# The down projection of a decoder layer: two of three token tiles by seven block products a unit, taken by groups of chunks

## The reference

```python
up = rmsnorm(x, g_ffn) @ w_up
upc, ffn_buf_new = causal_conv(ffn_buf, up, ffn_conv_w)
u, gt = jnp.split(upc, 2, axis=-1)
x = x + (jax.nn.silu(gt) * u) @ w_down        # w_down: 2816 x 1024
...
y_prompt = rmsnorm(xp, g_final)
```

## Time and profile before

| | us |
|---|---|
| median of 3 runs | 1082.9 |
| the profiled execution, its own time | 1084.21 |
| the profiled execution, span from first to last instruction | 1082.5 |
| up stage, products of L2078 | 378.8 to 814.4 |
| down stage, plain pairs of L2102 | 814.4 to 1041.1 |
| last pair and final norm | 1041.1 to 1082.5 |

### The profile page before, as it was taken

One profiled execution on the slowest core, in us unless ns is written; L12 is line 12 of the kernel. 1 busy time (PEld: TensorE's weight loads), 2 busy tenths in 40 slices (PEclk: granted clock), 3 DMA queues, 4 the chain that ended last, 5 costly groups with the idle time before them and its releaser, 6 DMA issues.

```text
span 1082.5 us, 17576 instructions
## 1 busy us (share of the span) xinstructions
PE 1060.4 (98%) x6746; PEld 1029.0 (95%) x6746; DVE 787.0 (73%) x1310; ACT 512.0 (47%) x880; POOL 43.5 (4%) x165
## 2 busy tenths in 40 slices
PE   7999999999999999999999999999999999999995
PEld 7999988888999999999999999999999999999994
DVE  6954788898899987778778768777777454454457
ACT  7444345665444554454454444444445333333354
POOL 0100000000000000000000000000000000000004
PEclk9999999999999999999999999999999999999998
DMA  7211201113544113112212211311336867556404
GB/s 259 96 40 45 97 21 40 38 61 144 152 130 141 62 59 118 59 59 98 78 59 84 93 59 62 115 59 60 106 128 210 285 199 221 178 180 198 146 1 157
DMA packets 47395, 119.09 MB, mean 110 GB/s; under 512 B 5040, under 2 KB 25392, under 8 KB 47280
## 3 DMA queue, kind: packets, MB, share of 16 engines
q1 hardware_dynamic: 43904, 113.59, 31.8%
q10 hardware_dynamic: 3408, 4.38, 1.1%
HBM read 98.33 MB, written 20.66 MB: 110 GB/s over the span
## 4 chain that ended last, share of the span: by engine, by line
PE 65%; DVE 4%; issue 2%; ACT 1%; DVEq 0%; ACTq 0%
PE psum L2078 40%; PE psum L2102 21%; PE psum L2054 2%; PE psum L1833 1%; DVE x_sb L1488 1%; DVE zb L1145 1%; DVE zb L1787 0%; PE psum L2135 0%; DVE att L1481 0%; DVE x_sb L1495 0%; DVE h_lo L1499 0%; DVE x_sb L1505 0%; ACT psum L1100 0%; DVE act_lo L1151 0%; DVE h_lo L1453 0%
## 5 line engine op out<-in xcount | busy, mean ns | idle before, releaser
L2078 PE MATMUL psum<-h_hi,w_lo 128*128 128x344 f32 x336 | 107.4, 320 | 0.0
L2078 PE MATMUL psum<-h_hi,act_lo 128*128 128x344 f32 x336 | 107.3, 319 | 0.0
L2078 PE MATMUL psum<-h_hi,act_hi 128*128 128x344 f32 x336 | 107.3, 319 | 0.0
L2078 PE MATMUL psum<-h_hi,w_hi 128*128 128x344 f32 x336 | 107.3, 319 | 0.0
L2078 PE MATMUL psum<-h_lo,act_hi 128*128 128x344 f32 x336 | 107.2, 319 | 0.0
L2078 PE MATMUL psum<-h_lo,w_hi 128*128 128x344 f32 x336 | 107.1, 319 | 0.0
L1151 DVE TENSOR_TENSOR w_lo<-raw,w_hi 128x1024 fp32r<-128x1024 f32 x50 | 61.1, 1224 | 59.8 <-ACT w_hi L727 59.7
L727 ACT ACTIVATE w_hi<-raw 128x1024 fp32r<-128x1024 f32 x51 | 53.8, 1056 | 83.5 <-PE psum L2102 63.5
L2102 PE MATMUL psum<-h_hi,act_hi 128*128 128x344 f32 x240 | 77.1, 321 | 0.0
L2102 PE MATMUL psum<-h_hi,w_hi 128*128 128x344 f32 x240 | 76.9, 320 | 0.0
L2102 PE MATMUL psum<-h_lo,w_hi 128*128 128x344 f32 x240 | 76.7, 320 | 0.0
(11 more groups left out here) (313 smaller groups left out, 3033.3 us busy)
## 6 DMA issues: line engine op xcount, KB each, us to landing
raw<-in_w SPq DMA_DIRECT2D x111, 512.0 KB, 3.7
att<-in_w SPq DMA_DIRECT2D x26, 512.0 KB, 4.5
act_d<-att SPq DMA_DIRECT2D x20, 516.0 KB, 2.7
zb<-act_d SPq DMA_DIRECT2D x30, 344.0 KB, 4.2
x_sb<-in_x SPq DMA_DIRECT2D x8, 516.0 KB, 5.0
x_d<-x_sb ACTq DMA_DIRECT2D x12, 344.0 KB, 2.5
x_sb<-x_d SPq DMA_DIRECT2D x3, 1376.0 KB, 7.9
out_y<-x_sb SPq DMA_DIRECT2D x12, 344.0 KB, 2.5
```

The costliest lines, as they stand in the source:

```text
L2078: ins = mm(bank[to], a, b, start=(fresh and k == p == 0), stop=(k == HALF - 1 and p == 2), skip_group_check=True)
```

## The change

Tiles 0 and 1 of the down projection are made by seven block products, tile 2 stays plain. The 11 chunk pairs form three groups of 4, 3 and 4 pairs.

- A **unit** u is one group and two row blocks m: it loads two slots (first chunks and second chunks of the group's pairs, two row blocks wide), forms four weight sums, splits seven weight parts, and makes seven products of 3 x (pairs in the group) matmuls. It uses three banks; p1 is copied with its sign changed by ScalarE into the second bank (`preload`), and VectorE reads six times into `x_sb` (`s_read`). 12 units in all.
- A **T pair** tp is tile 2, plain, for one group and two row blocks: two slots, two banks, two reads. 12 in all.
- The order is T 0-3, units 0-3, T 4-5, units 4-7, T 6-7, units 8-11, T 8-11.
- The data of a group are nine operands (b11, b21, b22, D1 to D4, and two halves of tile 2), each in two **items**; 54 items of up to 344 KB go through the same three stage buffers. All activations are stored, with the differences: `pair_diffs` makes these on VectorE (four instructions of 344 columns a pair), and the store has three rows of 516 KB a pair. The weight loads now read runs of 256 floats instead of whole rows of 1024.
- The final norm of tiles 0 and 1 runs inside units 8-11, that of tile 2 at the end.

The core of the diff, with the order of each engine around the first units:

```diff
+GROUP_PAIRS = (4, 3, 4)
+T_PAIRS = (range(0, 4), range(4, 6), range(6, 8), range(8, 12))
+S_UNITS = (range(0, 4), range(4, 8), range(8, 12), range(0))
+S_ORDER = ("p1", "p5", "p6", "p2", "p7", "p3", "p4")
...
 sync engine
-            for i in range(3):
-                load_act(i)
-            for i in range(2, DOWNS + 1):
...
+            for n in range(4):
+                load_item(n)
+            for q in (4, 5, 6):
+                load_down(q)
+            load_item(4)
+            load_item(5)
+            load_down(7)
+            store_pair(NG - 1)
+            load_item(6)
+            load_item(7)
+            load_down(8)
+            sp.wait_ge(act_stored, 32 * NG)
+            sp.wait_ge(state_out, 2 * NF)
+            sp.dma_start(x_sb[:, :, tile(2)], x2_d[:, :, tile(2)]).then_inc(x2_last_back, 16)
+            for n in range(8, 18):
+                load_item(n)
+                if n in (9, 11, 13):
+                    load_down(9 + (n - 9) // 2)
+                if n in (12, 15):
+                    load_x2((n - 12) // 3)
...
+            def load_item(n):
+                if n < 3:
+                    sp.wait_ge(part_lo_ready, parts_by(NF - 1))
+                else:
+                    sp.wait_ge(act_split, n - 2)
...
 ScalarE
+            t_hi(2, 0)
+            item_hi(4)
+            item_hi(5)
...
+            s_hi(0, "a11")
+            s_hi(0, "S1")
+            item_hi(12)
+            item_hi(13)
+            s_hi(0, "S2")
+            s_hi(0, "a12")
+            item_hi(14)
+            item_hi(15)
+            item_hi(16)
+            item_hi(17)
+            s_hi(0, "S3")
+            s_hi(0, "S4")
+            nc.scalar.activation(small[:, 62:63], eps[:, 0:1], ACT.Sqrt)
+            for g in range(3):
+                for u in S_UNITS[g]:
+                    s_hi(u, "a22")
+                    preload(u)
...
 VectorE, last chunk of the up stage
-                    w_lo_ffn(DOWN_SLOT0)
+                    item_lo(0)
+                    t_lo(0, 0)
                 act_mult(n - 1)
                 read_v3(n)
...
 VectorE, last unit of groups 0 and 1
+                        s_read(u, "p5")
+                        t_lo(T_PAIRS[g + 1][0], 0)
+                        s_read(u, "p6")
+                            item_lo(item + 2)
+                            item_lo(item + 3)
+                        s_read(u, "p2")
+                            item_lo(item + 4)
+                            item_lo(item + 5)
+                        t_lo(T_PAIRS[g + 1][0], 1)
+                        s_read(u, "p7")
...
 VectorE, between groups
+                    unit_sums(u)
+                    item_lo(item + 2)
+                    item_lo(item + 3)
+                    for n, part in ((4, "a11"), (5, "S1")):
+                        item_lo(item + n)
+                        s_lo(u, part)
+                    t_read(ta, 0)
+                    t_read(ta, 1)
...
 TensorE
+            def s_product(u, p):
+                pe.wait_ge(down_lo, SPLIT_N["S", u, part])
+                if u % 4 == 0:
+                    pe.wait_ge(act_split, X_N[group_of(u), x, 1])
+                if p == "p1":
+                    pe.wait_ge(down_read, BANK_FREE["S", u, 0])
+                if p == "p5":
+                    pe.wait_ge(down_read, BANK_FREE["S", u, 2])
+                if p == "p6":
+                    pe.wait_ge(preloaded, u + 1)
+                if p in ("p7", "p3", "p4"):
+                    pe.wait_ge(down_read, READ_N["S", u, {"p7": "p6", "p3": "p5", "p4": "p7"}[p]])
```

More of the change, by code:

```diff
@@ new lines, in numbered, with group_of, t_place, s_output @@
+def numbered(items):
+    return {x: n + 1 for n, x in enumerate(items)}
+def group_of(n):
+    return n // 4
+def t_place(tp):
+    f = next(f for f in range(4) if tp in T_PAIRS[f])
+    return f, tp - T_PAIRS[f][0]
+def s_output(u, p):
+    m1, m2 = 2 * (u % 4), 2 * (u % 4) + 1
+    return {"p2": (m1, 0), "p6": (m1, 1), "p3": (m1, 1), "p5": (m2, 1), "p7": (m2, 1), "p4": (m2, 0)}[p]
+LOADS = phases(lambda tp: [("T", tp, c) for c in range(2)], lambda u: [("S", u, c) for c in range(2)])
+LOAD_AT = numbered(LOADS)
@@ new lines, with halves_of, split_used @@
+X_ITEMS = x_items(0, T_X) + x_items(0, S_X) + x_items(1, T_X) + x_items(1, S_X) + x_items(2, S_X) + x_items(2, T_X)
+X_N = numbered(X_ITEMS)
+def halves_of(split):
+    kind, n, x = split
+    if kind == "S":
+        return (S_PARTS.index(x),)
+    e = (2 * t_place(n)[1] + x) % 4
+    return 2 * e, 2 * e + 1
+def split_used(split):
+    kind, n, x = split
+    if kind == "T":
+        return DONE_N["T", n, ("c0", "m1")[x]]
+    return DONE_N["S", n, next(p for p in S_ORDER if PRODUCTS[p][0] == x)]
@@ new lines, in home_free, with bank_free @@
+def home_free():
+    user, free = {}, {}
+    for split in SPLITS:
+        free[split] = max(split_used(user[h]) if h in user else 0 for h in halves_of(split))
+        for h in halves_of(split):
+            user[h] = split
+    return free
+def bank_free():
+    last, free = {}, {}
+    for key in phases(lambda tp: [("T", tp, i) for i in range(2)], lambda u: [("S", u, b) for b in range(3)]):
+        kind, n, i = key
+        b = T_BANKS[n][i] if kind == "T" else S_BANKS[n % 2][i]
+        free[key] = last.get(b, 0)
+        last[b] = READ_N[key] if kind == "T" else READ_N["S", n, ("p2", "p4", "p3")[i]]
+    return free
@@ L248, in landed_at @@
 def landed_at(s):
-    return 16 * sum(raw_of(r) == raw_of(s) for r in range(s + 1))
+    return 16 * sum((2 if r >= DOWN_SLOT0 and group_of(LOADS[r - DOWN_SLOT0][1]) == 2 else 1)
+                    for r in range(s + 1) if raw_of(r) == raw_of(s))
 def split_at(s):
@@ L1130, in _ @@
+            for m in (4, 5):
+                last_gain(m)
+            last_square(6)
+            last_square(7)
+            last_gain(6)
+            fin_root(2)
+            last_gain(7)
         @block.vector
@@ L1757, in _ @@
                 else:
-                    act_rest(1)
+                    t_lo(0, 1)
+                    item_lo(3)
                 read_c21(n)
@@ L1762, in _ @@
                 else:
[L1763 removed]
+                    t_lo(1, 0)
+                if n % 2 == 0:
+                    pair_diffs(n // 2 - 1)
             read_c12(NF - 1)
             tap_1(NF - 1, 1)
[L1766 removed]
+            t_lo(1, 1)
             tap_2(NF - 1, 1)
@@ L1813, in _ @@
-            fin_add(NT - 1, 5)
-            dve.wait_ge(fin_rstd_ready, NT - 1)
+            pair_diffs(NG - 1)
+            t_lo(2, 0)
+            item_lo(4)
+            item_lo(5)
+            t_lo(2, 1)
+            item_lo(6)
+            item_lo(7)
+            t_lo(3, 0)
+            item_lo(8)
+            item_lo(9)
+            t_lo(3, 1)
+            unit_sums(0)
+            item_lo(10)
+            item_lo(11)
+            for i in range(2):
+                t_read(0, i)
+            s_lo(0, "a11")
@@ new lines, in _ @@
+            last = S_UNITS[2][-1]
+            ta, tb, tc, td = T_PAIRS[3]
+            t_lo(tb, 0)
+            mid_add(last, "p3")
+            mid_add(last, "p4")
+            t_lo(tb, 1)
+            t_read(ta, 0)
+            t_read(ta, 1)
+            fin_reciprocal(0)
+            t_lo(tc, 0)
+            last_add(1)
+            fin_reciprocal(1)
+            t_lo(tc, 1)
+            t_read(tb, 0)
+            t_read(tb, 1)
+            t_lo(td, 0)
+            last_add(2)
+            last_add(3)
@@ L2110, in _, with fin_sum @@
+            def fin_sum(total, first, last):
+                return mm(task_ps[:, 0:TW], ones[:, :], total, start=first, stop=last)
             for name in FIRST_ORDER:
```

775 lines of the change are left out of this document (528 added, 247 removed).

## The result

The changed kernel takes **1099.9 us** (median of 4, 1099.3 to 1101.4), the one before 1082.7 in the runs beside it: 1.0159 times as long, 95% interval 1.0142 to 1.0177. Forecast were 1087.5 us and a range of 1075 to 1098. The direction was right; +4.6 us became +17.2.

A forecast was written before the change was run, and what follows sets the result against it. It took TensorE's unbroken run of matmuls to bound the kernel. Savings of 20.8 and 5.4 us against 0.7 + 1.7 + 16.8 + 2.2 + 8.9 + 0.5 added gave +4.6 us, 1087.5 us on the median, range 1075 to 1098.

The forecast's parts named there:

- The matmuls and the tail: Down stage: 132 fewer matmuls at 157.4 ns save 20.8 us; a shorter end after the last products saves 5.4 us.
- (a): Last chunk of the up stage: VectorE's added splits ahead of read_v3 delay p4 by 1.7 us, bounds 0 and 3.
- Units: Steady units: VectorE's and ScalarE's added work is hidden by matmuls; 0.7 us in all, bounds 0 and 6.
- rival 2: Down-stage units: VectorE becomes the bound, 0.8 us of waits in 12 units, +10 us, 1097; chance 0.12.
- Rival 3: Down-stage weight loads: 1024 B runs double a slot's queue time, 1096; sign: over 5 us landing in a quiet queue; chance 0.07.
- Rival 1: Queue between 828 and 860: waits overlap or are shorter, items 6 to 17 land by 852, 1076.5 us; chance 0.31.
- (b): First units: items behind the last pair's store in a full queue make TensorE wait 16.8 us, bounds 10 and 21.
- the walk: First units, item by item: landing is issue + 2.1 us + bytes/380 KB/us, or the previous landing + bytes/380.
- (c): Change from group 0 to 1: waits in units 3 and 4 for VectorE's reads, 2.2 us, bounds 0 and 5.
- (d): Change from group 1 to 2: waits in units 7 and 8 for items and reads, 8.9 us, bounds 4 and 13.
- (e): Clock: TensorE's slower matmuls after stalls fall mostly into waits that follow anyway; 0.5 us, bounds 0 and 4.

The follow-up runs named there:

- run 4: Changed kernel with p7's read in units 3 and 7, and splits and T-pair reads between groups, ahead of items: 1099.4 us, ratio 1.0152 to the kernel before.
- run 9: Changed kernel with the load of x2 for tile 2 queued behind items 8 and 9 instead of ahead of item 8: 1098.5 us, ratio 1.0141 to the kernel before.
- Runs 5 and 6: Each against the changed kernel: T pair 3's weight splits and unit 0's first splits ahead of later items, 1099.95 us; a fourth buffer for items, 1090.3 us.
- run 1: Changed kernel with short fp32 matmuls filling TensorE's idle at five waits, no wait shortened, output wrong: 1101.4 us, ratio 1.0171 to the kernel before.
- the best version: Changed kernel with four item buffers and reordered splits and reads, including reads, sums and splits ahead of items between groups: 1079.4 us, ratio 0.9967 to the kernel before.
- run 2: Changed kernel with VectorE's first two down splits of the last up chunk moved behind act_mult and read_v3: 1097.2 us, ratio 1.0132 to the kernel before.

## Why the prediction was wrong

*The matmuls and the tail.* 132 fewer at 157 ns, as forecast: between 877.0 and 914.8 there are 240 in 37.78 us. From T pair 0's start at 818.2 to the end at 1099.7 are 281.5 us. Less 228.5 of matmuls, 28.4 of waits, 1.5 of restarts behind them and 7.8 of slow matmuls, 15.3 stay for sums and tail, where 13.4 were forecast and 18.8 are there before. The gain was 3.5, not 5.4.

*(a)* 2.3 for 1.7. *Units:* rival 2 did not come; VectorE is busy for 31.8 of 40 us in steady units and TensorE never waits. *Rival 3* neither: from 877 us on the weight loads of 384 KB in 1 KB runs land in 3.5 us, those of 512 KB in 4 KB runs before the change in 3.6 (medians), where rival 3 asked for over 5. The Trainium skill's rule (Perfetto Trace Analysis, DMA Optimizations) speaks of DMAs below 2 KB; read as a rule on the runs inside a large transfer, it is not borne out here at 1 KB. *Rival 1:* the waits did not overlap, and item 17 came at 866, not by 852.

***(b)* is the step that failed**: "Walking through it item by item: [...] 17 at 860", and with it p7 of unit 0 at 870.7. It was 877.0, 6.3 us late: half of the 12.6 us by which the span of 1087.1 was missed. By item 17 it is 6.1: 2.4 are the later store (0.6 from (a), 1.6 from the slow matmuls behind it; in run 4, without these, the store is 0.6 late in all), 0.9 its way and item 6's, 1.4 the way from item 6 to item 8, and 1.5 the buffers from item 8 to 14 that VectorE frees late because it has sums and weight splits ahead of the item's split. The 1.4 are not the place of `x2` in the queue: run 9 takes it away from there, and item 8 still comes 4.7 us behind item 6, where the walk's rule gives 3.2. The queue moved less than the 380 KB/us of the walk; why stays open. The Trainium skill's figures in the prediction (DMA: Bandwidth & Descriptors, Anatomy of one DMA) would have made this step worse, and they are a fit for transfers that GpSimd issues; these are issued by the sync engine.

That the length of the idle came out right (9.5 for 9.3) hid this: TensorE arrived late, too. Runs 5 and 6 show it: taking away 5.7 us of waits in T pair 3 left p6's instant where it was and gained nothing, a fourth buffer gained 9.6. The total of 30.7 for 30.3 is partly luck as well: T pair 3 waited 5.7 us for 3.1, p1 of unit 0 none for 1.8, p7 of unit 0 1.2 for 2.6, p4 of unit 3 2.3 for 0.9, p7 of unit 8 none for 1.3.

*(c), (d)* The forecast's instants for the next waits, counted on from 870.7, are 915.0, 935.2, 972.3 and 988.1 us; they were 922.85, 943.4, 980.8 and 1000.0. So unit 3 adds 1.5 to the delay (2.3 for 0.9), units 4 and 7 add 0.7, p1 of unit 8 adds 3.4, and the end 0.7. In the account 2.4 of the 3.4 are slow matmuls behind p4 of unit 7; but in run 1, which has none there, p1 starts at the same instant (1000.1).

*(e)* was 0.5 and stands in the account with 9.4. Among the terms of the sum it is the one missed by most: 8.9 of the 12.6, beside 1.9 of the tail, 1.5 of restarts, for which the forecast had no term, and 0.4 of waits. As an account this closes the sum; as a cause it does not. Run 1 took away 6.3 of it on balance and gained nothing, as the product behind waited for VectorE's read or split instead. The one stretch whose slip is seen handed on is the first, ahead of the store: without it the store and `preload(0)` come 1.3 and 1.2 us earlier in run 1, and 1.9 and 1.3 in run 4, which is not edited up to there. "This falls mostly into waits that follow anyway" was right; what it fell into were waits whose ends had been put too early.

What stays open: what the single shares of buffers and orders are inside the 17.3 us (they were tried only in these combinations), why the queue between items 6 and 8 moved less than forecast, and the 13.9 us of waits that the best version still has.

## What to carry to other kernels

Forecast instants, not lengths of stalls: for each buffer write down when the engine that frees it gets there in its own order, with all that stands ahead. A stall that is followed by a longer wait for the same source costs nothing and its removal gains nothing; look for the last one, and for the resource whose instants it repeats (here the items' buffers and VectorE's list). A stall ahead of what starts the supply, like the first one here ahead of the store, is the exception (run 2). When a change turns one long accumulation into groups with a change-over between them, price the change-over by the busiest helper engine, and give it one buffer more than its steady state needs.
